# Gate and up products of a two-layer encoder: one 512-column product over tokens and their rests, on one core

## The reference

```python
h = rmsnorm(x, norm_ffn)
ff = jax.nn.silu(h @ w_gate) * (h @ w_up)
return x + ff @ w_down
```

## Time and profile before

| | |
|---|---|
| median of 3 runs | 1264.53 us (1263.86 to 1264.61) |
| profiled execution | 1263.36 us, span 1261.6 us |
| busy, share of the span | PE 98%, PEld 85%, DVE 56%, ACT 54%, POOL 53% |
| mean granted TensorE clock | 0.999 |
| DMA | 115.99 MB, mean 92 GB/s |

### The profile page before, as it was taken

The page is one execution under the profiler, slowest core; times in us unless marked ns, Lnnn a source line. Parts: engine busy times, 40 slices in busy tenths (PEclk is TensorE's granted clock), DMA queues, the critical chain, the costliest instruction groups (busy, mean ns, idle before and its releaser), DMA issues.

```text
span 1261.6 us, 23375 instructions
## 1 busy us (share of the span) xinstructions
PE 1236.0 (98%) x9232; PEld 1072.2 (85%) x9232; DVE 701.7 (56%) x1110; ACT 683.6 (54%) x1342; POOL 672.6 (53%) x484
## 2 busy tenths in 40 slices
PE   7999999999999999999999999999999999999997
PEld 6767787879999999888877777788899999998886
DVE  6845576677776777300058465665877767750003
ACT  6756655448665555432256766554576555553233
POOL 3745752557465354666626776338364433346662
PEclk9999999999999999999999999999999999999999
DMA  6211211232222222332222212214122233323232
GB/s 249 84 52 52 68 51 68 73 145 90 101 102 101 101 101 84 118 100 97 89 72 78 68 51 68 69 51 150 51 85 101 101 108 116 113 85 111 91 99 84
DMA packets 31501, 115.99 MB, mean 92 GB/s; under 512 B 3488, under 2 KB 3872, under 8 KB 31008
## 3 DMA queue, kind: packets, MB, share of 16 engines
q1 hardware_dynamic: 31392, 114.49, 26.5%
HBM read 112.37 MB, written 2.10 MB: 91 GB/s over the span
## 4 chain that ended last, share of the span: by engine, by line
PE 86%; DVE 6%; ACT 4%; issue 2%; POOL 1%; DMA 1%; POOLq 0%; SPq 0%; ACTq 0%; DVEq 0%
PE ps L1998 11%; PE ps L2001 10%; PE ps L2000 10%; PE ps L1855 6%; PE ps L1857 6%; PE ps L1877 6%; PE ps L1874 6%; PE ps L1875 6%; PE ps L1856 6%; PE ps L2157 2%; PE ps L2143 2%; PE ps L1871 2%; PE ps L1866 2%; PE ps L1868 2%; POOL w_lo L1175 1%
## 5 line engine op out<-in xcount | busy, mean ns | idle before, releaser
L1175 POOL TENSOR_TENSOR w_lo<-w_raw,w_hi 128x1024 fp32r<-128x1024 f32 x108 | 265.2, 2457 | 295.7 <-ACT w_hi L686 238.8
L686 ACT ACTIVATE w_hi<-w_raw 128x1024 fp32r<-128x1024 f32 x108 | 114.0, 1056 | 186.4 <-PE ps L1877 170.8
L1998 PE MATMUL ps<-h_hi,w_hi 128*128 128x256 f32 x672 | 191.0, 284 | 0.0
L2000 PE MATMUL ps<-h_lo,w_hi 128*128 128x256 f32 x672 | 190.1, 283 | 0.0
L2001 PE MATMUL ps<-h_hi,w_lo 128*128 128x256 f32 x672 | 190.1, 283 | 0.0
L1855 PE MATMUL ps<-h_hi,w_hi 128*128 128x512 f32 (+1 forms) x392 | 166.3, 424 | 1.4 <-DVE g L1604 0.7
L1998 PE MATMUL ps<-sum_hi,w_hi 128*128 128x256 f32 x528 | 150.2, 284 | 3.6 <-DVE silu L1406 2.2
L1857 PE MATMUL ps<-h_hi,w_lo 128*128 128x512 f32 (+1 forms) x392 | 152.0, 388 | 0.0
L1856 PE MATMUL ps<-h_lo,w_hi 128*128 128x512 f32 (+1 forms) x392 | 151.2, 386 | 0.0
L2000 PE MATMUL ps<-sum_lo,w_hi 128*128 128x256 f32 x528 | 149.4, 283 | 0.0
L2001 PE MATMUL ps<-sum_hi,w_lo 128*128 128x256 f32 x528 | 149.3, 283 | 0.0
(11 more groups left out here) (277 smaller groups left out, 2823.7 us busy)
## 6 DMA issues: line engine op xcount, KB each, us to landing
w_raw<-in_units SPq DMA_DIRECT2D x110, 512.0 KB, 3.5
u<-in_pairs SPq DMA_DIRECT2D x44, 512.0 KB, 4.3
w_raw<-in_pairs SPq DMA_DIRECT2D x40, 512.0 KB, 4.3
gain<-in_gain SPq DMA_DIRECT2D x5, 512.0 KB, 4.3
par<-in_par SPq DMA_DIRECT2D x2, 1214.5 KB, 6.2
x<-in_x SPq DMA_DIRECT2D x4, 512.0 KB, 7.1
spec<-in_pairs SPq DMA_DIRECT2D x4, 512.0 KB, 5.1
out_y<-x SPq DMA_DIRECT2D x3, 512.0 KB, 2.6
```

The lines of the kernel that those rows point to most:

```text
L686: nc.scalar.activation(w_tile(g, 0), w_raw[:, g % RAW], ACT.Copy).then_inc(s_hi, 1)
L1175: nc.gpsimd.tensor_tensor(w_tile(g, 1), w_raw[:, g % RAW], w_tile(g, 0).bitcast(F32), ALU.subtract).then_inc(s_lo, 1)
L1998: nc.tensor.matmul(out, hi[:, cols], factor[m][0][:, k], start=start and k == 0, stop=False, skip_group_check=True)
L2000: nc.tensor.matmul(out, hi[:, cols], factor[m][1][:, k], start=False, stop=False, skip_group_check=True)
```

## The change

From p = `WIDE` = 4 on, h_hi and h_lo (and sum_hi, sum_lo) lie in one tile, and the first two matmuls of each k become one of 512 columns, whose moving operand is 256 rounded columns followed by 256 columns of rests. The third (weight rests by rounded tokens) still has 256 columns. The result is two halves of a PSUM bank that have to be added later, the fold. `copy_m1`, `copy_u2`, `copy_u3` and the three sums on DVE (`gate_first`, `up_second`, `up_first`) handle 512 columns; four folds of 256 columns per p run on POOL; a new `copy_gate` brings the m4 bank to SBUF; `silu_second` runs on its fold. m2 gets bank 5, which the filter network used. `filter_half` uses bank 5 for both ways with signed tiles of full depth, and `window_half` writes both ways in one instruction, so `window_sums` goes except for a one-row sum.

```diff
+WIDE = 4
...
+        def both(m, p):
+            bank = SPARE if m == "m2" else fourth_bank(p) if m in ("m5", "m3") else chain_bank(p)
+            return ps[:, bank, :]
...
             def copy_u2(L, p):
                 act.wait_ge(prod_done.sem, prod_done.at(L, NUMBER["m6", p] + 1))
+                if p >= WIDE:
+                    act.wait_ge(hid1d.sem, hid1d.at(L, p - 1))
...
+                    nc.scalar.activation(wide_u2(p), both("m6", p), ACT.Copy).then_inc(u2c.sem, 1)
...
             def silu_first(L, p):
-                act.wait_ge(gate1.sem, gate1.at(L, p + 1))
+                if p >= WIDE:
+                    act.wait_ge(g1f.sem, g1f.at(L, p - WIDE + 1))
...
+            def copy_gate(L, p):
+                act.wait_ge(prod_done.sem, prod_done.at(L, NUMBER["m4", p] + 1))
+                act.wait_ge(hid2d.sem, hid2d.at(L, p - 1))
+                nc.scalar.activation(wide_gate(p), both("m4", p), ACT.Copy).then_inc(g2c.sem, 1)
+
             def silu_second(L, p):
+                if p >= WIDE:
+                    act.wait_ge(g2f.sem, g2f.at(L, p - WIDE + 1))
+                    nc.scalar.activation(wide_gate(p)[:, FIRST], wide_gate(p)[:, FIRST], ACT.Silu).then_inc(silu2.sem, 1)
+                    return
...
                     copy_u2(L, p)
+                    if p - 1 >= WIDE:
+                        silu_second(L, p - 1)
                     hi_item(L, NUMBER["m4", p])
...
-                    silu_second(L, p)
+                    if p >= WIDE:
+                        copy_gate(L, p)
+                    else:
+                        silu_second(L, p)
...
+            def fold_first_gate(L, p):
+                pool.wait_ge(gate1.sem, gate1.at(L, p + 1))
+                pool.wait_ge(hid1d.sem, hid1d.at(L, p - 2))
+                nc.gpsimd.tensor_tensor(silu[:, p % 3], m1w[:, p % 2, FIRST], m1w[:, p % 2, SECOND], ALU.add)\
+                    .then_inc(g1f.sem, 1)
...
+            def fold_second_gate(L, p):
+                pool.wait_ge(g2c.sem, g2c.at(L, p - WIDE + 1))
+                t = wide_gate(p)
+                nc.gpsimd.tensor_tensor(t[:, FIRST], t[:, FIRST], t[:, SECOND], ALU.add).then_inc(g2f.sem, 1)
...
                     if not rest_on_vector(j):
                         lo_item(L, j)
-                    m, p = ITEMS[j]
+                    if m == "m3" and WIDE <= p < LAST:
+                        fold_second_up(L, p)
+                    if m == "m1" and p - 1 >= WIDE:
+                        fold_first_gate(L, p - 1)
+                    if m == "m2" and p - 2 >= WIDE:
+                        fold_second_gate(L, p - 2)
+                        fold_first_up(L, p - 2)
...
+                    if p - 1 >= WIDE:
+                        hidden_second(L, p - 1)
+                        hidden_first(L, p - 1)
                     if L + 1 < DEPTH and p in F_HALVES:
-                        window_half(L + 1, p, *F_HALVES[p])
+                        window_half(L + 1, *F_HALVES[p])
                     up_second(L, p)
...
-                    hidden_second(L, p)
+                    if p < WIDE:
+                        hidden_second(L, p)
...
+                    elif p >= WIDE + 2:
+                        pe.wait_ge(g2c.sem, g2c.at(L, chain_before(p) - WIDE + 1))
...
                 for k in range(KT // 2):
                     cols = slice(P * k, P * k + P)
-                    nc.tensor.matmul(out, hi[:, cols], factor[m][0][:, k], start=start and k == 0, stop=False,
-                                     skip_group_check=True)
-                    nc.tensor.matmul(out, hi[:, cols], factor[m][1][:, k], start=False, stop=False, skip_group_check=True)
-                    last = nc.tensor.matmul(out, lo[:, cols], factor[m][0][:, k], start=False, stop=k == KT // 2 - 1,
+                    if p >= WIDE:
+                        nc.tensor.matmul(both(m, p).rearrange("p (v t) -> p v t", v=2), hi[:, cols], factor[m][:, :, k],
+                                         start=start and k == 0, stop=False, skip_group_check=True)
...
+                    last = nc.tensor.matmul(both(m, p)[:, FIRST] if p >= WIDE else out, lo[:, cols], factor[m][:, 0, k],
+                                            start=False, stop=k == KT // 2 - 1,
                                             skip_group_check=True)
```

More of the change, by code:

```diff
@@ L730, in copy_m1 @@
             def copy_m1(L, p):
+                if p >= WIDE:
+                    act.wait_ge(prod_done.sem, prod_done.at(L, NUMBER["m1", p] + 1))
+                    act.wait_ge(gate1.sem, gate1.at(L, WIDE))
+                    if p >= WIDE + 2:
+                        act.wait_ge(g1f.sem, g1f.at(L, p - 2 - WIDE + 1))
+                    nc.scalar.activation(m1w[:, p % 2], both("m1", p), ACT.Copy).then_inc(m1c.sem, 1)
+                    return
                 act.wait_ge(prod_done.sem, prod_done.at(L, NUMBER["m2", p] + 1))
@@ L743, in copy_u3 @@
                 act.wait_ge(prod_done.sem, prod_done.at(L, NUMBER["m7", p] + 1))
+                if p >= WIDE:
+                    if p == WIDE:
+                        act.wait_ge(xsd.sem, xsd.at(2 * L + 2, 0))
+                    act.wait_ge(hid2d.sem, hid2d.at(L, p - 1))
+                    nc.scalar.activation(u3w[p % 2], both("m7", p), ACT.Copy).then_inc(u3c.sem, 1)
+                    return
                 if p >= 2:
@@ L1405, in gate_first @@
                 v.wait_ge(m1c.sem, m1c.at(L, p + 1))
-                nc.vector.tensor_tensor(silu[:, p % 3], direct(p), m1_of[:, p % 3], ALU.add).then_inc(gate1.sem, 1)
+                to, part, m1 = (silu[:, p % 3], direct(p), m1_of[:, p % 3]) if p < WIDE else \
+                    (m1w[:, p % 2], both("m2", p), m1w[:, p % 2])
+                nc.vector.tensor_tensor(to, part, m1, ALU.add).then_inc(gate1.sem, 1)
             def up_second(L, p):
@@ L1411, in up_second @@
                 v.wait_ge(u3c.sem, u3c.at(L, p + 1))
-                nc.vector.tensor_tensor(up2[:, p % 2], fourth(p), u3[:, p % 2], ALU.add).then_inc(up2d.sem, 1)
+                to, part, u3_of = (up2[:, p % 2], fourth(p), u3[:, p % 2]) if p < WIDE else \
+                    (u3w[p % 2], both("m5", p), u3w[p % 2])
+                nc.vector.tensor_tensor(to, part, u3_of, ALU.add).then_inc(up2d.sem, 1)
             def up_first(L, p):
@@ L1912, in net_one @@
                     pe.wait_ge(s_feat, 16)
-                nc.tensor.matmul(ps[0:FFN_HY, net_bank(L, 0), 0:SEQ], par[0:EMB, C_W1:C_W1 + FFN_HY], feat, start=True,
+                nc.tensor.matmul(ps[0:FFN_HY, net_bank(L, 0), SECOND if L else FIRST], par[0:EMB, C_W1:C_W1 + FFN_HY], feat, start=True,
                                  stop=True).then_inc(net.sem, 1)
@@ L1947, in filter_half @@
                 at = C_W3 + o * HY + SEQ * n
-                outs = (ps[:, SPARE, FIRST], ps[:, fourth_bank(p), SECOND])
-                for way in range(2):
-                    rows = slice(FFN_HY * way, FFN_HY * way + FFN_HY)
-                    last = nc.tensor.matmul(outs[way], hid_a[rows, t:SEQ:2], par[rows, at:at + SEQ], start=way == 0,
-                                            stop=True, skip_group_check=True)
+                for cols, signed in ((FIRST, hid_a), (SECOND, hid_m)):
+                    last = nc.tensor.matmul(ps[:, SPARE, cols], signed[:, t:SEQ:2], par[:, at:at + SEQ], start=True,
+                                            stop=True)
                 last.then_inc(abp.sem if n else wayp.sem, 1)
```

155 lines of the change are left out of this document (114 added, 41 removed).

## The result

The changed kernel takes 1395.9 us (median of 4 runs, 1393.45 to 1397.2); the kernel before, run beside it, 1264.19 us. The ratio is 1.1039, 95% interval 1.1024 to 1.1055: slower by 10.4%. The forecast was 1379 us, range 1358 to 1408. The profiled execution took 1393.45 us, with a span of 1391.7 us; that is 130.1 us more than the profiled 1263.36 of before, where the sum gave 115.3. It is the fastest of the four; their mean granted clocks run from 0.981 down to 0.975.

What follows compares the result with a forecast made beforehand. A 12.94 us loop per step through ACT, DVE and POOL, not PE, was taken to bound the kernel. 1263.36 + 50.6 (layer 1) + 64.7 (layer 0) = 1378.7, forecast 1379 us, range 1358 to 1408.

Steps and rivals of the forecast that it cites:

- The loop through the other engines: Gate and up steps: chain through ACT, DVE and POOL closes once per step, 12.94 us against a 10.09 us step before.
- 50.6 per layer: Gate and up stage: added us in each layer from longer steps, beginning, hidden tile's rests and end; layer 0 has more.
- The sixteen transitions: Steps from p = 4 to 20: 2.85 us more each, 45.6; hidden tile's rests on POOL add 0.78 four times, 3.1.
- The end: Last tile of each layer: changed order behind silu_first and its fold starts m7(21) later, 2.4 us more.
- A reduction: Layer 0, POOL: each range reduction stands inside the loop, adding 7.1 us at p = 6 and 6.6 at p = 9.
- the scalar operations: Layer 0, DVE: two scalar operations ahead of outer_sums add 0.5 us each, 1.0 in all.
- A filter step: Layer 0's eight filter steps: chain from window product through PE takes 13.6 to 13.7 us, against 10.90 before.
- PE's granted clock falls: Rival: idle gaps drop PE to 1.2 GHz and it binds again, 1587 us; chance 0.03.
- The tail costs nothing: Down projection: last tile's folds end before PE's third token tile reads them, so nothing is added.
- DVE and POOL block each other: Rival: hidden products with two SBUF inputs meet POOL's work, on average 1.0 us more per turn, 1411 us; chance 0.09.
- PE needs 0.36 us less per step: PE: merged matmuls save 0.051 us per product, 9.73 us per step; 12.8 us in all if PE stays the bound.
- PE stays the bound: Rival: the loop through the other engines closes in under 9.73 us, so the kernel gets faster, 1251 us; chance 0.05.

Runs made afterwards that it cites:

- the last kernel: All the order edits combined on the changed kernel, with layer 0's network matmuls behind m6 and the last tile's old ACT order: 1258.45 us, ratio 0.9954.

## Why the prediction held, point by point

- *The loop through the other engines is 12.94 us.* Right: 12.86. The links stood where they were put (12.58 for the end of the gate's fold against 12.51), and moving single ones shortened the step to what was expected: 12.10 with the gate's fold ahead of the rest of m2, 11.35 with `silu_second` late.
- *50.6 per layer at the ends and in the loop.* Right for layer 1, 50.1, though two terms within were off in opposite ways. The sixteen transitions cost 44.9 (11.87, 13.53, 13.53, 13.01, and twelve of 12.86, less 16 of 10.09) where 48.2 was forecast, for 1.6 of it because the hidden tile's rests lengthened three steps by 0.67, 0.67 and 0.15, not four by 0.78, and for 1.3 because a step is 12.86, not 12.94. The end cost 5.2, not 2.4; the last step was 14.42.
- *A reduction adds 7.1 and 6.6, the scalar operations 1.0.* The reductions are right: 7.2 and 6.0. The scalar operations are not. Their two steps are 13.57 and 13.80 now, 0.7 and 0.95 above their like in layer 1, but before the change they were 10.89 and 10.81 against 10.08. So they add about 0.1 to the difference, not 1.0. A third step, from m7(5) to m7(6), took 10.84 before, so that it grew by 0.8 less than its like in layer 1; the sum had no term for this.
- *A filter step is 13.6 to 13.7.* This term was mis-sized: 15.43. It was the largest miss, some 14 us over eight steps, and about 15 in the sum, since the last of the eight took 10.17 before the change, not 10.90. PE's part in the chain was counted at full clock. In these steps alone PE is in the chain (m2, m4, m3, the pair, m6 stand behind the window product) and has just idled 3 us. The rival "PE's granted clock falls" was rejected for the whole and was true for seven of these eight. Filling the wait took out 1.35 us per step; 0.4 stay unexplained.
- *The tail costs nothing.* Wrong by 3.6 us in all. The folds do end in time, but the hidden product behind the last fold was counted at 0.42, where POOL's next rest stretches it to 2.51. PE's wait for it is 3.1 of the 3.6. The rival "DVE and POOL block each other" was right at this place and wrong in the loop, where rows of the changed kernel show 0.41 and 0.42, for the reason given: POOL is idle there.
- *PE needs 0.36 us less per step.* Mis-sized for most steps: 0.19 to 0.20 in layer 1. Three steps of layer 0 in the last kernel do reach the forecast (9.71, 9.71 and 9.75). It changed nothing in the forecast, since PE isn't the bound, but it is the prize: near 7 us, not 12.8.
- *"PE stays the bound", 1251 us.* It takes the moves of order above to get there, and then it is 1258.45, not 1251.

So 1378.7 + 11.7 (layer 0) - 0.5 (layer 1) + 3.6 (the rest) is 1393.5, and the profiled execution took 1393.45. That the whole is off by no more than the filter steps alone is in part luck: the filter steps cost about 15 more than the sum had, the rest of the program 3.6 more, and against that layer 0 came out 3.1 lower in its scalar steps, its reductions and its end, and the loops of the two layers 1.0 lower.
